# One near product of banded queries and levels in key blocks, with smaller first transfers

## The reference, cut to what matters

```python
def step(S, inp):
    q_, k_, g_, v_ = inp
    o_inter = jnp.einsum('bhtk,bhkv->bhtv', q_ * jnp.exp(g_), S)
    diff = g_[:, :, :, None, :] - g_[:, :, None, :, :]
    decay = jnp.where(mask, jnp.exp(jnp.where(mask, diff, 0.0)), 0.0)
    a = jnp.einsum('bhtk,bhtsk,bhsk->bhts', q_, decay, k_)
    o = o_inter + jnp.einsum('bhts,bhsv->bhtv', a, v_)
```

## Time and profile before

| | us |
|---|---|
| median of 3 runs | 2190.28 |
| lowest, highest | 2186.19, 2190.56 |
| the profiled execution's own time | 2185.88 |
| its span | 2184.1 |
| PE busy | 2148.8 (98%) |
| DVE busy | 1220.6 (56%) |
| ACT busy | 801.1 (37%) |

### The profile page before, as it was taken

How to read it: one execution, slowest core, us unless ns; L and a number is a source line. 1 busy time by engine, 2 the same in 40 slices (tenths; PEclk the granted TensorE clock), 3 DMA queues, 4 the chain that set the end, 5 groups by cost and what they waited for, 6 DMA issues and landing times.

```text
span 2184.1 us, 27326 instructions
## 1 busy us (share of the span) xinstructions
PE 2148.8 (98%) x9916; PEld 1764.0 (81%) x9916; DVE 1220.6 (56%) x1986; ACT 801.1 (37%) x990; POOL 341.8 (16%) x179
## 2 busy tenths in 40 slices
PE   8999999999999999999899999999999999999998
PEld 7888878888888888788688778888888788886887
DVE  5224464554645646436733388888888764466332
ACT  3224364453544645312622232222323442126221
POOL 0000000000000000000300024444757430003000
PEclk9999999999999999999999999999999999999999
DMA  8222221122122212422233322222222234221331
GB/s 317 80 97 77 78 78 69 66 77 77 58 77 77 77 64 77 148 96 96 78 120 120 120 93 96 97 97 96 96 96 97 94 115 155 96 96 58 127 121 60
DMA packets 31551, 213.77 MB, mean 98 GB/s; under 512 B 3744, under 2 KB 3744, under 8 KB 7296
## 3 DMA queue, kind: packets, MB, share of 16 engines
q1 hardware_dynamic: 26928, 189.80, 24.3%
q0 software_dynamic: 4560, 23.20, 2.7%
HBM read 204.60 MB, written 8.39 MB: 98 GB/s over the span
## 4 chain that ended last, share of the span: by engine, by line
PE 95%; ACT 2%; DVE 1%; issue 1%; DMA 0%; POOL 0%; SPq 0%; DVEq 0%; ACTq 0%; POOLq 0%
PE G L419 86%; PE X L419 7%; PE T L419 1%; PE T L558 1%; ACT w_hi L769 1%; ACT Y L997 1%; DMA Z<-xT_in 0%; DVE w_lo L1117 0%; ACT a_hi L773 0%; DVE a_lo L1122 0%; POOL a_lo L340 0%; PE T L663 0%; DVE tmp L1472 0%; ACT Z L934 0%; DVE Y L1501 0%
## 5 line engine op out<-in xcount | busy, mean ns | idle before, releaser
L419 PE MATMUL G<-a_hi,w_hi 128*128 128x512 f32 (+1 forms) x2784 | 1092.4, 393 | 21.3 <-POOL a_lo L340 10.9
L419 PE MATMUL G<-a_lo,w_hi 128*128 128x512 f32 (+1 forms) x2784 | 1081.5, 389 | 0.0
L419 PE MATMUL G<-a_hi,w_lo 128*128 128x512 f32 x2752 | 1074.0, 390 | 0.0
L769 ACT ACTIVATE w_hi<-w_raw 128x2048 fp32r<-128x2048 f32 x175 | 335.1, 1915 | 1107.4 <-PE G L419 1103.1
L1117 DVE TENSOR_TENSOR w_lo<-w_raw,w_hi 128x2048 fp32r<-128x2048 f32 x128 | 293.5, 2293 | 691.8 <-ACT w_hi L769 691.8
L419 PEld LDWEIGHTS G<-a_hi,w_hi 128*128 128x128 f32 x2784 | 524.6, 188 | 138.9 <-POOL a_lo L340 16.2
L419 PEld LDWEIGHTS G<-a_lo,w_hi 128*128 128x128 f32 x2784 | 524.8, 189 | 107.7 <-issue 1.5
L419 PEld LDWEIGHTS G<-a_hi,w_lo 128*128 128x128 f32 x2752 | 518.2, 188 | 109.1
L1638 DVE SCALAR_TENSOR_TENSOR T<-tmp,par,T 128x512 f32<-128x512 f32 x464 | 306.9, 748 | 0.0
L363 POOL TENSOR_TENSOR w_lo<-w_raw,w_hi 128x2048 fp32r<-128x2048 f32 x46 | 212.5, 4619 | 247.8 <-ACT w_hi L769 247.8
L334 POOL DMA_DIRECT2D Y<-xT_in x4 | 2.1, 532 | 848.0 <-DVE a_lo L1122 848.0
(11 more groups left out here) (234 smaller groups left out, 1438.0 us busy)
## 6 DMA issues: line engine op xcount, KB each, us to landing
w_raw<-wall_in SPq DMA_DIRECT2D x175, 1024.0 KB, 4.8
Z<-xT_in SPq DMA_DIRECT2D x4, 1024.0 KB, 11.3
Y<-w_in POOLq DMA_DIRECT2D x2, 2048.0 KB, 18.9
Y<-xT_in POOLq DMA_DIRECT2D x4, 1024.0 KB, 5.0
x_residual<-Y POOLq DMA_DIRECT2D x16, 256.0 KB, 3.8
Y<-x_residual POOLq DMA_DIRECT2D x4, 1024.0 KB, 5.8
out<-Y POOLq DMA_DIRECT2D x16, 256.0 KB, 3.6
w_raw<-wall_in SPq DMA_DIRECT2D x8, 256.0 KB, 10.3
```

What stands on the lines that cost most here:

```text
L419: return pe.matmul(o, l, r, start=start, stop=stop)
L769: f(w_hi[:, w.slot, :], w_raw[:, w.slot, :], ACT.Copy).then_inc(S("w_hi"), 1)
```

## The change

The recurrence: the levels 4 and 2 are gone, and the near part covers distances 0 to 7 inside blocks of 8 tokens. For each distance n the queries are multiplied with exp(g[t] - g[t-n]), and lie side by side in a new buffer `qb`: for each of 16 blocks of 32 tokens, 4*(8-n) columns for distance n, 144 in all (`BAND_AT`). One product of a block's 32 keys with its 144 columns gives all distances of that block; DVE picks the entries out with 8 masks (`take_near`). Level 64 stays in its place; levels 32, 16 and 8 run at the head's end, each in blocks of their own key columns, with output rows at the block's place.

The start: x arrives in ten pieces (`X_PIECES`), the first two issued by ACT; tile 1's lag grows from 2 to 6 (`START_LAG`); tile 2 is loaded and split in quarters; three more matmuls of warm-up. `square_sums(HEADS)` runs behind step 4 instead of 2. Some buffers are laid on others (`nmx`, `rg`, `stat`), and the scratch for POOL's transfers is 1024 instead of 4096.

```diff
-WARM_UP = 14
+WARM_UP = 17
+X_PIECES = tuple((k, k + 1) for k in range(4)) + tuple((k, k + 2) for k in range(4, 16, 2))
+START_LAG = (2, 2, 2, 2, 2, 2, 3, 3, 3, 4, 4, 5, 5, 5, 6, 6)
-HALVES = (64, 32, 16, 8, 4, 2, 1)
+HALVES = (64, 32, 16, 8)
+BLOCK = 32
+NEAR = 8
+BAND_AT = tuple(sum(BLOCK // NEAR * (NEAR - m) for m in range(n)) for n in range(NEAR + 1))
@@ SP
-                sp.dma_start(w_raw[:, 0, quarter(q)], wall[0][:, quarter(q)]).then_inc(S(quarter_landed(0, q)), 16)
-                sp.dma_start(Z[:, at], xT[:, at]).then_inc(S(f"x_landed{q}"), 16)
-                sp.dma_start(w_raw[:, 1, quarter(q)], wall[1][:, quarter(q)]).then_inc(S(quarter_landed(1, q)), 16)
-            sp.wait_ge(S("w_split"), 1)
-            sp.dma_start(w_raw[:, 0, :], wall[2]).then_inc(S("w_landed0"), 16)
+                first_w(0, q)
+                first_x(2 * q + 2)
+                first_w(1, q)
+                first_x(2 * q + 3)
+            for q in range(4):
+                sp.wait_ge(*((S("quarter_split"), 2 * q + 1) if q < 3 else (S("w_split"), 1)))
+                sp.dma_start(w_raw[:, 0, quarter(q)], wall[2][:, quarter(q)]).then_inc(S(quarter_landed(0, q)), 16)
@@ PE
-                        last = mm(NEAR_BANKS[c // 2][:, at:at + P + HALF], kk[:, cs], qp[:, c, :])
-                    last = mm(bank[0:rows, at + c * HALF:at + (c + 1) * HALF], keys[:, 0:rows], queries)
+            def near_products(h):
+                pe.wait_ge(S("level_ready"), h * LEVELS + 1)
                 for c in range(NT):
+                    for b in range(P // BLOCK):
+                        rows = slice(b * BLOCK, (b + 1) * BLOCK)
+                        keys = kk[:, c * P + b * BLOCK:c * P + (b + 1) * BLOCK]
+                        last = mm(near[rows, c, :], keys, qb[:, c * (P // BLOCK) + b, :])
+            def level(h, e):
+                width = max(2 * half, BLOCK)
+                used = width - half
+                    for lo in range(0, P, width):
+                        last = mm(out[lo:lo + used, c, :], keys[:, lo:lo + used], queries)
-                for l in range(3):
-                    level(h, l)
+                near_products(h)
+                level(h, 0)
-                pe.wait_ge(S("level_copied"), h * COPIES + 2)
-                for l in range(3, LEVELS):
-                    level(h, l)
+                for e in range(1, len(HALVES)):
+                    level(h, e)
-            second_part(0, {2: last_square})
+            second_part(0, {4: last_square})
@@ ACT
+            for n in range(2):
+                act.dma_start(Z[:, at], xT[:, at]).then_inc(S(f"x_landed{n}"), 16)
+                if i == 1:
+                    act.wait_ge(S("gemm_done"), 1)
+                    for q in range(4):
+                        split_quarter(0, q, 2)
-                for e in range(-1, 3):
-                    decay(e)
+                decay_bands(1, 3)
+                decay_bands(3, NEAR)
+                decay(0)
@@ DVE
+                    for n in BANDS[1:]:
+                        tt(band(n), g[:, :, :, n:NEAR], g[:, :, :, 0:NEAR - n], ALU.subtract).then_inc(S("gap"), 1)
+                        last = tt(band(n), band(n), band(0)[:, :, :, n:NEAR], ALU.mult)
```

More of the change, by code:

```diff
@@ L100, in constants @@
     masks = np.zeros((P, MASKS), np.float32)
[L101 to L105, removed]
+    s, u = np.arange(P)[:, None] % BLOCK, np.arange(BLOCK)
+    for n in BANDS:
+        masks[:, BAND_AT[n]:BAND_AT[n + 1]] = s == u[u % NEAR >= n] - n
+    second = u[u % (2 * NEAR) >= NEAR]
+    masks[:, NEAR_COLS:] = (s // (2 * NEAR) == second // (2 * NEAR)) & (s % (2 * NEAR) < NEAR)
     return cols, masks
@@ L445, in gemm_pair @@
             def gemm_pair(w, g, acts, between=None, quarters=False):
+                seconds = 0
                 for k in range(KC + LAG):
-                    for n, kn in ((0, k), (1, k - LAG)):
-                        if not 0 <= kn < KC:
-                            continue
+                    lag = START_LAG[k] if quarters and k < KC else LAG
+                    steps = [(0, k)] if k < KC else []
+                    while seconds <= k - lag and seconds < KC:
+                        steps.append((1, seconds))
+                        seconds += 1
+                    for n, kn in steps:
                         wn, gn = Idx(w + n), Idx(g + n)
@@ L919, in head @@
                 f(kpT[:, 0:3 * P], kpT[:, 0:3 * P], ACT.Exp).then_inc(S("decay_k"), 1)
-                for e in range(3, 6):
+                for e in range(1, len(HALVES)):
                     decay(e)
@@ L1166, in _ @@
             for i in range(1, 13):
-                if i == 11:
+                if i == 1:
+                    for q in range(4):
+                        split_quarter(0, q, 6)
+                elif i == 11:
                     split_gates(Idx(12))
@@ new lines, in take_near @@
+                    for n in BANDS:
+                        src = near[:, :, BAND_AT[n]:BAND_AT[n + 1]].rearrange("p c (s n) -> p c s n", n=NEAR - n)
+                        m = mask(BAND_AT[n], BAND_AT[n + 1], NEAR - n)
+                        if n == 0:
+                            last = tt(sums, src, m, ALU.mult)
+                        else:
+                            wait_alone(("near_copied", h * 9 + n))
+                            last = dve.copy_predicated(sums[:, :, :, n:NEAR], m, src)
+                        last.then_inc(S("near_copied"), 1)
@@ new lines, in take_blocks @@
+                def take_blocks(e):
+                    dve.wait_ge(S("level_done"), h * LEVELS + min(e, 1) * (LEVELS - 2) + 2)
+                    half = HALVES[e]
+                    src = LEVEL_OUT[e].rearrange("p (c n) -> p c n", c=NT)
+                    for lo in range(0, P, 2 * half):
+                        rows = slice(lo, lo + half)
+                        last = dve.tensor_copy(AT.rearrange("p (c n) -> p c n", c=NT)[rows, :, lo + half:lo + 2 * half], src[rows, :, :])
+                    last.then_inc(S("level_copied"), 1)
@@ L1417, in head @@
                    ALU.subtract).then_inc(S("gap_k"), 1)
-                gap(3)
-                dve.wait_ge(S("level_done"), h * LEVELS + 3)
-                for e in range(4, 6):
+                for e in range(1, len(HALVES)):
                     gap(e)
```

202 lines of the change are left out of this document (109 added, 93 removed).

## The result

| | before | after |
|---|---|---|
| median, us | 2188.59 (4 runs) | 2158.97 (4 runs) |
| lowest, highest | 2186.19, 2190.56 | 2155.81, 2160.60 |
| profiled execution, its own time | 2185.88 | 2159.29 |
| its span | 2184.1 | 2157.6 |

The ratio is 0.9864, with a 95% interval of 0.9849 to 0.9880: the change makes the kernel 29.6 us faster by the medians and 26.6 us by the two profiled executions. The prediction said 2170; the measured time lies 0.03 us under the low end of its range.

A forecast was written before the change was run, and what follows sets the result against it. PE bounds the kernel, busy 98% of the span and 95% of the chain. From 2185.9 us, 13.4 us for eight heads and 3.5 us for the start give 2169.0, plus a little over 1 us: 2170 us, range 2159 to 2192.

The forecast's parts named there:

- the price of a narrow record: PE's records with 32, 24 or 16 weight columns: taken as 32 ns each, 33 ns for the near products.
- near and level 64, a head: PE's near products and level 64 in mid-head: from 2.7 us to 1.85 us, a gain of 0.85 us a head.
- last cluster, a head: PE's small level products at a head's end: 3.49 us to 2.66 us for 80 records, gain 0.83 us.
- wait behind the last head: PE's 1.06 us wait for L1217, behind DVE's taking and a copy: claimed to grow by 1.3 us.
- squares: Moving `square_sums` by two steps lets PE do 6 matmuls, 1.36 us, inside its wait of 2.32 us.
- Rival (a): Narrow records in each head: price keeps falling with width, 2.8 us gained a head, about 2161 us; chance 0.20.
- Rival (b): Narrow records in each head: price never falls below 56 ns, 8 us lost, 2190 by the median; chance 0.16.
- (d): Narrow records in each head: a price between, about 44 ns, gaining 0.2 us a head, 2181 us; chance 0.09.
- Rival (c): Near products: four strips do not overlap as two do, 120 ns a record, 1.9 us lost a head, 2192; chance 0.11.
- Part 3: DVE and ACT work inside the heads: DVE 3.05 us each for gaps and scaling, cover 4.8 us, cost nothing.
- Part 4: Behind the last head: wait for L1217 grows 1.3 us, 1.36 us of matmuls fill the squares' wait, together 0.
- Part 5: The start: earlier first matmul 1.5, clock 1.4, stalls 0.2, third tile 0.8, less 0.4 us; 3.5 us taken, bounds 1.5 to 4.5.

## Why the prediction was wrong

The sign and the places of the gain were right. The size was not, nor was the reason given for the price of a narrow record: 16.9 us forecast from the profiled execution's time, 26.6 us measured.

| term, us saved, between the two profiles | forecast | measured |
|---|---|---|
| near and level 64, a head | 0.85 | 0.98 |
| last cluster, a head | 0.83 | 2.16 |
| the rest of a head, by difference | 0 | -0.15 |
| eight heads | 13.4 | 23.9 |
| start | 3.5 | 5.2 |
| wait behind the last head | -1.3 | -1.6 |
| squares | 1.4 | 1.4 |
| clock behind the last head, in the convolutions | 0 | -3.2 |
| behind the last output transfer | 0 | 1.6 |
| scattered | 0 | -0.7 |

**The step that failed is the price of a narrow record**, "I take 32 ns for every narrow record". It is 10 ns in the mean, and 17 ns with the gap behind the 80. The prediction had drawn from the earlier trace rows that two neighbouring strips work at the same time, and for the near products it divided by four strips: 30 ns for the stream, 33 ns taken, 34.7 ns measured. For the levels it didn't: there it took the width of one record's weights as if the next load had to wait for it. In one strip it does, with 25 to 32 ns; across two strips a record costs 16 ns and across four 9 ns. By its own rule for streams the lower bound was 28/4 = 7 ns, and 80 x 7 = 0.6 us should have stood in the range. With that bound the low end would have been some 16 us lower than the forecast's 2170 for this term alone. The sentence "no gain below it, since two instructions have to be fed for each" was a guess without a row, and 10 ns refutes it. The forecast erred by 1.33 x 8 = 10.6 us here.

**Two smaller terms.** The start saved 5.2 us between the two profiles, outside its bounds of 1.5 to 4.5. And the smaller scratch for POOL's transfers was put at nothing; the 1.6 us behind the last output transfer may be its work, which stays open.

**Rival (a)** named a last cluster of 1.7 us and 2161 us in all, and was nearest. Its reason is not the one: in one strip 16 and 24 columns cost the same 25 ns. Rival (b), 56 ns, and (d), 44 ns, are out by the timeline. By the prediction's own terms (6.19 us before, 112 records and 0.89 us for the rest after) the 44 ns of (d) give a gain of 0.4 us a head, not 0.2, and 2180 us, not 2181. The Trainium skill, "TensorE: Matmul & The Clock Gate", Back-to-back issue gap, has the floor of about 62 ns per matmul where the sequencer decodes in software; neither cluster shows it (10 and 35 ns). Rival (c) is out: four strips overlap, and the order of the loops is what makes them do so.

**Part 3 was right.** DVE's seven gaps for the bands take 2.5 us and the seven scalings 2.5 us (forecast 2.4 each), its last scaling for level 64 ends at 305.8, 4.8 us before PE's near products begin, and these wait for nothing.

**Part 4 was right in its waits** (forecast 2.4 us, measured 2.68; for the squares about 1, measured 0.92) and missed what the longer wait did to the clock: 18 matmuls took 6.02 us instead of 4.40.

**Part 5.** The first gemm matmul came at 6.80, forecast 8.4: the first pieces landed sooner than I put them. The clock stayed at 1.00 as forecast; its part is 5.16 - 3.09 (first matmul) - 0.82 (third tile) + 0.12 (stalls 0.81 for 0.69) = 1.37 us, forecast 1.4. The third tile's wait is gone as forecast. But only 3.0 us of the 5.2 are the new start's by the run with the old start, which is near the 3.5 us forecast; where the other 2.2 us come from is open. In part, then, the agreement term by term is luck: in the run with the old start the clock did not fall, so the 1.4 us for it are not a steady gain.

**The range** missed at its low end since the bound on the narrow record was missing in it. The clock's 3.2 us went the other way: without them the miss would have been larger. The 2.2 us of the start and the 1.6 us at the end went with it: without those the time would have been within the range, with the price of a record just as wrong.

## What to carry to other kernels

A product with few key columns is worth cutting into strips of 32 output rows if consecutive matmuls go to different strips: put the strip's loop innermost (10 against 20 ns a record for the levels, 35 against 83 ns for the near products here). For a lower bound on a small record, divide one strip's time by the strips that take turns; two strips reached it here (32 to 16 ns), four did not quite (25 to 9 ns). Don't let a loop's pass end on a burst of the shortest records; a few slower ones behind it hide the late instructions (0.43 us a pass). When PE's work is made shorter at a place without cover, look at what frees its next bank, and put that ahead of everything else on its engine: one such move was worth 4.4 us, 2.7 for its wait and 1.6 for the clock.

## What the runs showed of the hardware

- On two strips in turn f32 records of 32 weight columns begin 16 ns apart, on four strips those of 16 and 24 columns 9 ns; in one strip it is 32 ns for 32 columns and 25 ns for 24 and for 16.
- Behind such a burst the next instruction is 0.29 to 0.38 us late, after 80 or 240 records, where another pass or loop follows: in six heads of eight, and not in the first, which is written out, nor in the last. Eight records of level 64 (0.6 us) behind the burst hide it, and with 20 or 28 ns a record it isn't there.
- With 240 records PE stood for 1.96 to 2.07 us inside the burst in three heads of eight, just those whose code it ran for the first time, with a packet on an instruction queue within 1 us of each stop's beginning.
- Behind the last head the granted clock fell after waits of 2.65 to 2.78 us in six executions (two of the changed kernel) and after 3.61 us in a seventh, and not after 2.7 us in the kernel with the old start, nor after 3.10 us in the one with level 64 last. At the start it stayed at 1.00 after 1.81 us, had fallen after 2.99 us, and fell after waits of 1.28 and 0.44 us with ten warm-up matmuls ahead. So the length of the one wait doesn't decide it alone. The same long gemm of the convolutions took 213.2 us in four of the twelve profiles and 214.7 to 214.8 us in the other eight.
- Right behind the near products and the narrow levels a gemm's 48 matmuls take 11.12 to 11.20 us instead of 10.98, by the chains of before and after.
- From the start of the last output transfer to the end of the span it was 4.5 us before and 2.9 us in the eleven other profiles.
